# The RWKV recurrence of a four-layer model: value share of the outputs behind the rest, next unit's first products one turn earlier, level products in both halves of one bank pair

## The reference

```
def step(state, inp):
    r_t, w_t, k_t, v_t, kk_t, a_t = inp
    sa = jnp.einsum('bhvk,bhk->bhv', state, -kk_t)
    state = (state * w_t[:, :, None, :]
             + sa[..., None] * (kk_t * a_t)[:, :, None, :]
             + v_t[..., None] * k_t[:, :, None, :])
    return state, jnp.einsum('bhvk,bhk->bhv', state, r_t)

state0 = jnp.zeros((bsz, H, N, N), f32)
_, y = lax.scan(step, state0, (tm(rh), tm(wh), tm(kh), tm(vh), tm(kk), tm(ah)))
y = tm(y)
mean = jnp.mean(y, axis=-1, keepdims=True)
var = jnp.mean(jnp.square(y - mean), axis=-1, keepdims=True)
y = ((y - mean) * lax.rsqrt(var + RW_GN_EPS)).reshape(bsz, seq, d) * ln_w + ln_b
bonus = jnp.sum(rh * kh * r_k, axis=-1, keepdims=True) * vh
out = ((y + bonus.reshape(bsz, seq, d)) * g).astype(h.dtype) @ w_o
```

## Time and profile before

| | us |
|---|---|
| three timed runs | 3115.61, 3127.9, 3129.53 |
| their median | 3127.9 |
| the profiled execution | 3120.45 |
| its span, first to last instruction | 3118.5 |
| turn n = 1, 2, 3 of the first pass | 21.20, 25.49, 28.65 |
| turn n = 1, 2, 3 of the second pass | 25.13, 22.85, 27.02 |

### The profile page before, as it was taken

How to read it: one execution, slowest core, us unless ns; L and a number is a source line. 1 busy time by engine, 2 the same in 40 slices (tenths; PEclk the granted TensorE clock), 3 DMA queues, 4 the chain that set the end, 5 groups by cost and what they waited for, 6 DMA issues and landing times.

```text
span 3118.5 us, 50917 instructions
## 1 busy us (share of the span) xinstructions
PE 3004.4 (96%) x20442; PEld 2643.3 (85%) x20442; DVE 2349.9 (75%) x3461; ACT 1392.9 (45%) x2214; POOL 97.3 (3%) x187
## 2 busy tenths in 40 slices
PE   7998989999999999999999999999999999999998
PEld 6896788888889888888896888887788888989887
DVE  6978865888877867879867887887854866665684
ACT  4534122544545753545444554544123544465453
POOL 0000000000000000000000000000000000000000
PEclk9999988999999999999999999999989999999899
DMA  8774433676666336675664666672302543444453
GB/s 345 260 296 152 155 113 132 239 285 248 230 263 239 111 117 234 243 281 214 256 237 156 252 239 249 232 276 89 115 22 82 201 184 123 163 162 145 160 188 129
DMA packets 69674, 609.51 MB, mean 195 GB/s; under 512 B 7728, under 2 KB 7888, under 8 KB 31824
## 3 DMA queue, kind: packets, MB, share of 16 engines
q1 hardware_dynamic: 42768, 459.41, 39.5%
q0 software_dynamic: 26352, 144.85, 12.3%
q10 hardware_dynamic: 336, 2.13, 0.2%
HBM read 604.26 MB, written 2.10 MB: 194 GB/s over the span
## 4 chain that ended last, share of the span: by engine, by line
PE 84%; DVE 9%; ACT 2%; DMA 2%; issue 1%; PEld 1%; PEldq 0%; SPq 0%; DVEq 0%; POOLq 0%; ACTq 0%
PE psum L325 25%; PE psum L928 23%; PE psum L932 12%; PE psum L949 10%; PE psum L956 6%; PE psum L323 4%; PE psum L953 2%; DMA weights<-in_weights 1%; DVE arena L814 1%; DVE arena L2345 1%; DVE ada_sum L507 1%; PE psum L1665 1%; DVE wkv_base L2087 1%; DVE small L2086 1%; PEld psum L325 1%
## 5 line engine op out<-in xcount | busy, mean ns | idle before, releaser
L879 ACT ACTIVATE unit_high<-weights 128x1024 fp32r<-128x1024 f32 x594 | 629.2, 1061 | 710.5 <-PE psum L932 390.0
L885 DVE TENSOR_TENSOR unit_low<-weights,unit_high 128x1024 fp32r<-128x1024 f32 x594 | 725.8, 1223 | 201.5 <-ACT unit_high L879 200.8
L928 PE MATMUL psum<-h_part,unit_high 128*128 128x512 f32 x3168 | 819.7, 396 | 22.0 <-DVE h_part L801 15.7
L928 PEld LDWEIGHTS psum<-h_part,unit_high 128*128 128x128 f32 x3168 | 575.6, 190 | 130.9 <-issue 18.1
L932 PEld LDWEIGHTS psum<-h_part,unit_low 128*128 128x128 f32 x3168 | 444.5, 192 | 29.5
L932 PE MATMUL psum<-h_part,unit_low 128*128 128x256 f32 x3168 | 465.9, 283 | 0.0
L325 PE MATMUL psum<-in_part,w_part 128*128 128x256 f32 x2784 | 359.9, 289 | 7.2 <-issue 4.1
L325 PEld LDWEIGHTS psum<-in_part,w_part 128*128 128x128 f32 x2784 | 347.0, 196 | 23.2 <-ACT arena L1207 11.1
L949 PE MATMUL psum<-hidden,unit_high 128*128 128x512 f32 x1386 | 354.0, 397 | 0.0
L1055 DVE TENSOR_REDUCE arena<-psum 128x256 f32<-128x512 f32 x396 | 272.9, 689 | 58.5 <-PE psum L932 47.2
L507 DVE SCALAR_TENSOR_TENSOR ada_sum<-ada_in,c_act,ada_sum 128x1536 f32<-128x1536 f32 x154 | 278.7, 1812 | 23.6 <-DMA ada_in<-in_ada_w 23.6
(11 more groups left out here) (314 smaller groups left out, 2769.3 us busy)
## 6 DMA issues: line engine op xcount, KB each, us to landing
weights<-in_weights SPq DMA_DIRECT2D x290, 1536.0 KB, 6.5
ada_in<-in_ada_w POOLq DMA_DIRECT2D x182, 768.0 KB, 5.8
consts<-in_consts POOLq DMA_DIRECT2D x1, 1668.0 KB, 15.3
x<-in_x SPq DMA_DIRECT2D x1, 1024.0 KB, 8.6
v_first<-arena ACTq DMA_DIRECT2D x1, 1024.0 KB, 4.9
arena<-v_first ACTq DMA_DIRECT2D x1, 1024.0 KB, 4.8
weights<-in_weights SPq DMA_DIRECT2D x1, 512.0 KB, 6.5
out<-x SPq DMA_DIRECT2D x1, 512.0 KB, 2.6
```

Source lines behind the costliest of these rows:

```text
L879: k.nc.scalar.activation(k.unit_part[0][:, n % UNIT_RING], w, ACT.Copy).then_inc(k.sem["unit_high"], 1)
L885: k.nc.vector.tensor_tensor(k.unit_part[1][:, n % UNIT_RING], w, k.unit_part[0][:, n % UNIT_RING].bitcast(FP32), ALU.subtract).then_inc(k. ...
L928: mm(k.psum[:, 2 * (j % 2) + half, :].rearrange("p (i t) -> p i t", i=2), lhsT=part(2 * j + half, 0, t), rhs=k.h_parts[:, :, t], start=t = ...
```

## The change

It doesn't add or remove any arithmetic. It does five things in the turns, and shifts the first unit's steps in the same way:

1. The value share (and state share) of the outputs leaves `upper` for a function of its own, `first_outs`, and stands straight behind `rest`, ahead of `upper`. So that both can be in PSUM at once, `rest` writes the tail's other bank pair.
2. `near_again` of unit n + 1 moves from the start of turn n + 1 into turn n, ahead of `keys`, and `level16` of the head opens the turn, ahead of `rest`.
3. Half products take a bank pair and a side: level16 and level32 in columns 0 to 255 of pair 0, x32 and y64 in columns 256 to 511 of the same pair, y32 in pair 1. `receptances` goes to pair 1 and behind `y64`; the wait for `out_read` goes from x32 to y32.
4. Head and tail steps alternate with an offset of one: `x32, across, y32, lower, level32, state_and_out, y64, receptances`.
5. On VectorE `variance` and `normed` of a tail leave the end of the turn and go into the next turn, behind `level16` there, with one modulation sum between them in the first pass; `turn_y` goes ahead of `receptances`; the last sums are spread over more places. The number of sums is the same.

```
-    def half_block(self, which, i, p, h):
-        at = self.bank(2 * which)
-        return self.k.psum[64 * h:64 * h + 64, at + i, p * 64:(p + 1) * 64]
+    def half_block(self, which, side, i, p, h):
+        at, to = self.bank(2 * which), 256 * side + p * 64
+        return self.k.psum[64 * h:64 * h + 64, at + i, to:to + 64]
...
     def x32(c):
         at("wk_t", c, 0, 2)
+        half_products(c, 0, 1, half_of(z.y[c.hf]), z.t[c.hf], s["wk_x32"])
+
+    def y32(c):
         if c.b:
             pe.wait_ge(s["wk_out_read"], UNITS * j + c.u - 1)
-        half_products(c, 1, half_of(z.y[c.hf]), z.t[c.hf], s["wk_x32"])
-
-    def y32(c):
-        half_products(c, 0, half_of(z.t[c.hf]), z.y[c.hf], s["wk_y32"])
+        half_products(c, 1, 0, half_of(z.t[c.hf]), z.y[c.hf], s["wk_y32"])
...
     def keys(c, between=lambda: None):
         for half in range(2):
             if half:
                 between()
+                at("wk_ra_read", c)
+            else:
                 at("wk_y", c, 1, 2)
-            else:
-                at("wk_ra_read", c)
...
-                ins = part(k.psum[:, c.bank(i), p * 64:(p + 1) * 64], lhsT=z.kl[c.hf][:, 4 * i + p, 1],
+                ins = part(k.psum[:, c.bank(2 + i), p * 64:(p + 1) * 64], lhsT=z.kl[c.hf][:, 4 * i + p, 1],
                            rhs=z.vt[:, c.b, 4 * c.hf + p, z.rows(i)], start=p == 0, stop=c.b == 0, skip_group_check=True)
...
                True, True, s["wk_sa"] if m == 7 else None)
+
+    def first_outs(c):
         for p in range(4):
             for i in range(2):
                 part(c.out(i, p), lhsT=z.kl[c.hf][:, 4 * i + p, 0], rhs=z.vt[:, c.b, 4 * c.hf + p, z.rows(i)],
...
     if j == 0:
         mod_sums(k, pe, pr, 2, range(6))
+    near_again(units[1])
+    if j == 0:
+        turn_mod_rows(k, pe, pr, 2)
     for n in range(1, UNITS):
         head, tail = units[n], units[n - 1]
-        if head.b:
-            pe.wait_ge(s["wk_sa_read"], 2 * (UNITS * j + head.u - 1))
-        near_again(head)
+        level16(head)
         rest(tail)
+        first_outs(tail)
         upper(tail)
         if n >= 2:
             turn_out(units[n - 2])
-        if n == 1 and j == 0:
-            turn_mod_rows(k, pe, pr, 2)
-        level16(head)
+        x32(head)
         across(tail)
         if n == 1 and j == 0:
             pe.wait_ge(s["mod_ready"], 3)
-        x32(head)
+        y32(head)
         lower(tail)
-        y32(head)
+        level32(head)
         state_and_out(tail)
-        level32(head)
+        y64(head)
         receptances(head)
-        if n == UNITS - 1:
+        if n + 1 < UNITS:
+            pe.wait_ge(s["wk_sa_read"], 2 * (UNITS * j + n))
+            near_again(units[n + 1])
+        else:
             early_outputs(0)
-        y64(head)
         keys(head)
...
         level16(head)
+        if n >= 2:
+            variance(chunks[n - 2])
+            beside()
+            normed(chunks[n - 2])
+        x32(head)
         across(tail)
-        x32(head)
         y32(head)
-        beside()
+        level32(head)
         if n >= 2:
             gated(chunks[n - 2])
         if n + 1 < UNITS:
             open_y(chunks[n + 1])
-        level32(head)
+        beside()
+        y64(head)
+        if n + 1 < UNITS:
+            turn_y(chunks[n + 1])
         receptances(head)
-        y64(head)
         keys(head, 0)
         keys(head, 1)
         centre(tail)
-        variance(tail)
-        normed(tail)
-        if n + 1 < UNITS:
-            turn_y(chunks[n + 1])
-        beside(2)
```

More of the change, by code:

```diff
@@ L1584, in near_again, with half_products @@
                    z.kk[z.rows(i), 4 * c.hf + p, z.now(c.b)], True, True, s["wk_near"] if p == 3 and i else None)
-    def half_products(c, which, left, right, signal):
+    def half_products(c, which, side, left, right, signal):
         for other in range(2):
@@ L1591, in half_products @@
                     i = h ^ other
-                    mm(c.half_block(which, i, p, h), left(4 * i + p, h), right[z.rows(h), 4 * i + p], True, True,
+                    mm(c.half_block(which, side, i, p, h), left(4 * i + p, h), right[z.rows(h), 4 * i + p], True, True,
                        signal if (other, p, h) == (1, 3, 1) else None)
@@ L1622, in receptances @@
             for i in range(2):
-                mm(c.pair(0)[:, 4 * i + p], z.a[z.rows(i), 4 * c.hf + p, z.now(c.b)],
+                mm(c.pair(1)[:, 4 * i + p], z.a[z.rows(i), 4 * c.hf + p, z.now(c.b)],
                    z.r[z.rows(i), 4 * c.hf + p, z.now(c.b)], True, True, s["wk_ra"] if p == 3 and i else None)
@@ L1653, in rest @@
             for i in range(2):
-                ins = part(k.psum[:, c.bank(i), p * 64:(p + 1) * 64], lhsT=z.kk[z.rows(i), 4 * c.hf + p, z.now(c.b)],
+                ins = part(k.psum[:, c.bank(2 + i), p * 64:(p + 1) * 64], lhsT=z.kk[z.rows(i), 4 * c.hf + p, z.now(c.b)],
                            rhs=z.state[z.rows(i), 4 * c.hf + p], start=False, stop=True, skip_group_check=True)
@@ L1732, in rw_products @@
     level32(head)
-    receptances(head)
     turn_ended(0)
     y64(head)
+    receptances(head)
     keys(head, lambda: turn_ended(1))
@@ L1897, in rest_read @@
         act_(z.res[c.hf].rearrange("p (i n) c -> p i n c", i=2),
-             k.psum[:, c.bank(0):c.bank(0) + 2, 0:256].rearrange("p i (n c) -> p i n c", n=4), f.Copy)\
+             k.psum[:, c.bank(2):c.bank(2) + 2, 0:256].rearrange("p i (n c) -> p i n c", n=4), f.Copy)\
             .then_inc(s["wk_res_read"], 1)
@@ L2184, in y32 @@
         at("wk_open", c)
[L2185 removed]
+        v.tensor_tensor(by_half(z.y[c.hf]), by_half(z.y[c.hf]), c.halves(1, 0), add).then_inc(s["wk_y"], 1)
     def level32(c):
         at("wk_lx", c, 1, 2)
[L2189 removed]
+        v.tensor_tensor(by_half(z.t[c.hf]), c.halves(0), each_half("level5"), mult).then_inc(s["wk_t"], 1)
     def receptances(c):
         at("wk_ra", c)
[L2193 removed]
+        v.tensor_tensor(z.rb[c.hf], c.pair(1), each("ssd_mask"), mult).then_inc(s["wk_ra_read"], 1)
     def y64(c):
@@ L2287, in rw_vector @@
         centre(tail)
-        variance(tail)
-        normed(tail)
-        if n + 1 < UNITS:
-            turn_y(chunks[n + 1])
-        beside(2)
+    variance(chunks[2])
+    beside()
+    normed(chunks[2])
     across(chunks[3])
+    beside(2)
     gated(chunks[2])
```

22 lines of the change are left out of this document (9 added, 13 removed).

## The result

The changed kernel's median is 3100.9 us (8 runs, 3098.28 to 3106.77) against 3123.39 us of the kernel before in the same rounds (8 runs): ratio 0.9931, 95% interval 0.9918 to 0.9944, by that ratio 21.5 us faster. The profiled execution took 3101.37 us, 19.1 us less than that of before; rival A had 3100.0 for it.

A forecast was written before the change was run, and what follows sets the result against it. TensorE, 84% of the chain, was taken to bound the kernel. 3120.45 - 3.0 (gaps) - 7.4 (clock) gives 3110.0 us; from the median of 3127.9 the same sum gives 3117.5; predicted the middle, 3113.5 us, range 3102 to 3126.

The forecast's parts named there:

- rival A: Clock holds in all six turns, all 17.5 us come back: 3100.0 us beside 3120.45; chance 0.20.
- The 0.69 us before `upper`: TensorE's wait for ScalarE's read of `rest` goes in all six turns, covered by the value share: -4.2 us.
- the 0.25 before `keys`: TensorE's wait for VectorE's mask of the receptances goes, covered by `near_again` and half of `keys`: -1.0 us.
- The new wait of `level16` in turn 1: Wait for ScalarE's `near_read`, 0.8 us in the first pass, 1.1 in the second; net +1.4 us.
- `turn_out` in turn 2: TensorE waits 0.4 us for `normed`, which now comes in the same turn, once per pass: +0.8 us.
- D: `turn_out` waits for a modulation sum's transfer in turns 2 and 3 of the first pass: 3125.4 us; chance 0.06.
- C: `rest` and value share in one slow piece make the clock fall in all six turns: 3126.5 us; chance 0.12.
- The 0.83 us before `rest`: TensorE's wait for VectorE's masks of the keys stays in turns 2 and 3 of both passes: no gain.
- Gaps: TensorE's waits in the six turns, all changes together: -3.0 us.
- The sums: VectorE's modulation sums, same number, transfers now issued one by one: put at nothing.
- The price: Time lost per us at half clock, from three pairs of turns (0.42, 0.38, 0.49): taken as 0.43.
- The clock: TensorE's granted clock in the turns: turn 3 keeps it in both passes, -7.4 us; the other turns stay as before.

The follow-up runs named there:

- part1_alone: The kernel before with only the value share put straight behind `rest`, which writes the tail's other bank pair: 3109.32 us, ratio 0.9966 to before.
- after_third: The changed kernel, unchanged, measured again as reference in later rounds: 3102.48 us, ratio 0.9924 to the kernel before.
- without_part1: The changed kernel with the value share back behind `upper`, all other moves kept: 3120.25 us, ratio 1.0 to the kernel before.
- gap_filled_short: The kernel before with three products that nobody reads between `rest` and `upper`: 3111.88 us, ratio 0.9975 to the kernel before.
- after_again: The changed kernel, unchanged, measured once more: 3097.76 us, ratio 0.9931 to the kernel before.
- rest_wait_shortened: The kernel before with the value share straight behind `rest`, plus one product that nobody reads ahead of `rest`: 3103.43 us, ratio 0.9952 to the kernel before.
- rest_wait_longer: The changed kernel with a small VectorE instruction more ahead of the masks: 3101.16 us, ratio 0.9943 to the kernel before.

## Why the prediction was wrong

*The 0.69 us before `upper`, the 0.25 before `keys`*: right, both waits are gone in all turns. *The new wait of `level16` in turn 1*: right, 0.8 and 1.2 us against 0.8 and 1.1. *`turn_out` in turn 2*: right, 0.40 and 0.41 against 0.4, by the mechanism named; rivals D (a transfer in the way) and C (falls everywhere) didn't come. What C leaned on was misread: `rest` and the value share aren't the slowest steps per instruction, 2.00 us for 16, as `turn_out` takes 0.66 us for 4 at the full clock (part1_alone, turn 2 of the first pass). *The 0.83 us before `rest`*: it stays, as said, but at 0.64 and 0.53 us; why it is shorter isn't worked out. Gaps: -3.8 us against -3.0. *The sums*, put at nothing, cost the new 1.6 us of `turn_out` behind the turns.

*The price*, 0.43 us per us at half clock: right (0.43 in part1_alone; after_third's turn 3, 28.05 against 22.17 us in its first pass for 13.5 us, is 0.44). One of the three pairs behind it was not a pair, though: turn 2 takes 22.41 us in the first pass and 21.19 in the second at the full clock (part1_alone), since VectorE's sums hold up the first, so its 0.38 isn't a price.

*The clock* is the step that failed: "Turn 2 has 0.83 and 0.4 us with some 5 us between them, nearest to the turns that fell; I let it fall as before. Turn 1 of the second pass has 1.1 us in one piece for 0.5 and 0.69: as before too". That left 10.1 + 10.2 + 3.2 = 23.5 us at half clock, and 3.5 were measured; 20.0 us x 0.43 = 8.6 us is as much as the miss between 3110.0 and 3101.37. (The middle of 3113.5 also leaned on a median of 3127.9 for the kernel before, which came to 3123.39 with more runs.) I treated a fall as settled by a turn's gaps and asked which turn looked like which. In its place the traces show a frequency: of the 12 turns of the two kernels with an idle gap before `upper` (before, without_part1) 11 fell, of the 108 turns of the 18 traces without it 9; in the two that only fill it, 3 of 12. Closing that gap thus kept most traced turns at 2.4 GHz beside the other short waits that these kernels have, and filling it with useless work (gap_filled_short) brought clock as well. By the medians it is about half of the clock's 17.5 us: 7.8 us in gap_filled_short, 10.6 less 2.2 of waits in part1_alone. The result is rival A, to which I gave 0.20, and the range ended at 3102 because I cut off its lower part. Luck is in it too: that the one fall of the first trace stood where I had let one stand (turn 2 of the second pass, 3.5 us for 3.2) didn't repeat in the other two traces, and turn 3, which I let keep the clock for its single gap, lost it for 13.5 us in after_third.

The second rule that the prediction weighed, of the Trainium skill ("TensorE: Matmul & The Clock Gate", section "A second HAM failure mode: psum-queue depth-cycling"), describes short idles between groups of products that make the clock swing; the 11 of 12 against 9 of 108 agree with it. The gap rule of the section "Why this matters for your kernels" of the same page of the Trainium skill speaks of idle times several times as long; by that, closing these gaps would have given no clock back, and the measurement (7.8 us from filling one) is against it.

What stays open: part1_alone brings 10.6 us and the changed kernel 21.5. Of the 10.9 between them 1.6 are waits (6.9 against 5.3). Some is neither wait nor clock: from `near_again` of unit 0 to the last `rest` a second pass without a fall takes 81.6 us in after_again and 83.1 in rest_wait_shortened, with the new order of the level steps in the first only. The shorter wait before `rest` may bring 4 to 7 us of clock, by the medians of the two kernels that shorten it. How the rest divides the runs don't settle.

## What to carry to other kernels

Ahead of any count of waits look at the granted clock of the stretch: here gaps of 9.1 us stood beside 40.8 us at half clock, an estimated 17.5 us more. Closing one of two short gaps a few us apart, by moving ready work into it, brought back about half of that. The other half came only together with the other moves, which alone brought nothing. Forecast it as a share of executions that fall, not turn by turn. And closing a gap alone brings out what it hides: VectorE's sums came out as a 1.24 us stall until they too were moved, and where they went they made one of 1.6 us.

## What was not expected of the hardware

The same program with the same waits lost the clock in none, one and two of six turns in three traces, in different turns, for 3.5 to 13.5 us at a time; its runs spread from 3092.49 to 3106.78 us. The falls are only a part of that spread: of the 13.7 us between the spans of after_again and after_third 7.4 lie in the six turns, and 4.8 ahead of the first one (start of its `rest` at 415.78 and 420.60). A VectorE instruction of 0.17 us ahead of the masks (rest_wait_longer) lengthened the wait behind them by 0.09 us only, as the next one started 0.09 us after it:

```profile
2290.77 0.17 DVE L2209 TENSOR_TENSOR norm_pair<-consts 128x16 f32<-128x16 f32 x1 [0.43 <-PE psum L325]
2290.86 2.48 DVE L2212 TENSOR_TENSOR arena<-psum,consts 128x512 f32<-128x512 f32 x4
```
